# A context tile taken out of the expert loop and gathered beside the latents' mixer

## What is computed

```python
h = rms_norm(x, g_norm1) * (1 + sc1) + sh1
x = x + ga1 * (concat(short_conv(h), bidirectional_mLSTM(h)) @ w_out)
h = rms_norm(x, g_norm2) * (1 + sc2) + sh2
# PEER, per token: 8 heads choose 16 of 16384 experts each
a = einsum('td,thkd->thk', h, u_tab[e])
x = x + ga2 * einsum('thk,thkd->td', gate * gelu(a), v_tab[e])
y = rms_norm(x, g_final)
```

## Time and profile before

| | us |
|---|---|
| median of 3 runs (lowest, highest) | 3864.77 (3859.73, 3868.69) |
| the profiled execution: its time | 3873.35 |
| its span, first to last instruction | 3871.2 |
| busy: PE, DVE, POOL, ACT | 3283.1, 2431.6, 1290.4, 978.3 |

### The profile page before, as it was taken

The page is one execution under the profiler, slowest core; times in us unless marked ns, Lnnn a source line. Parts: engine busy times, 40 slices in busy tenths (PEclk is TensorE's granted clock), DMA queues, the critical chain, the costliest instruction groups (busy, mean ns, idle before and its releaser), DMA issues.

```text
span 3871.2 us, 38481 instructions
## 1 busy us (share of the span) xinstructions
PE 3283.1 (85%) x10672; PEld 1647.3 (43%) x10672; DVE 2431.6 (63%) x6016; ACT 978.3 (25%) x2384; POOL 1290.4 (33%) x1174
## 2 busy tenths in 40 slices
PE   6999999479878888887888798788878878887887
PEld 4555555334434434443443344344334433443443
DVE  3433233466767766776677667666766767676776
ACT  1301101122322222232223222222222222222222
POOL 0000000144434443443444344344434434443443
PEclk8999999799999999999999899999999999999999
DMA  8010100799999999999999999999999999999998
GB/s 354 23 37 29 41 25 9 296 397 401 409 373 400 410 406 369 405 401 377 407 406 404 376 403 405 370 411 405 408 374 388 397 378 403 408 403 374 404 404 330
DMA packets 197995, 1298.57 MB, mean 335 GB/s; under 512 B 22336, under 2 KB 34944, under 8 KB 48768
## 3 DMA queue, kind: packets, MB, share of 16 engines
q0 software_dynamic: 165888, 1208.03, 77.0%
q1 hardware_dynamic: 31872, 87.83, 6.0%
HBM read 1285.76 MB, written 10.01 MB: 335 GB/s over the span
## 4 chain that ended last, share of the span: by engine, by line
DVE 23%; PE 20%; DMA 19%; issue 14%; ACT 3%; DVEq 2%; POOL 1%; ACTq 0%; POOLq 0%
DMA uv<-in_uv,expert 19%; PE acc L1062 15%; DVE uv L1250 8%; PE mix L1026 4%; DVE wt L1202 2%; ACT gelu L1112 2%; POOL uv L989 1%; DVE work L1186 1%; DVE work L1182 1%; DVE picked L1189 1%; ACT diag L1117 1%; DVE ind L1150 1%; DVE ind L1143 1%; DVE work L1144 1%; DVE pos L1165 1%
## 5 line engine op out<-in xcount | busy, mean ns | idle before, releaser
L1062 PE MATMUL acc<-uv,diag 128*128 128x512 f32 x4608 | 2210.9, 629 | 445.1 <-ACT diag L1117 445.0
L989 POOL DMA_INDIRECT uv<-in_uv,expert x1152 | 1286.8, 1117 | 1859.1 <-PE acc L1062 1588.5
L1250 DVE CUSTOM_DVE_ANT_0 uv<-uv,h 128x1024 f32<-128x1024 f32 x1152 | 1385.6, 1221 | 484.5 <-DMA uv<-in_uv,expert 481.3
L1062 PEld LDWEIGHTS acc<-uv,diag 128*128 128x128 f32 x4608 | 884.4, 199 | 1658.0 <-issue 966.4
L1117 ACT ACTIVATE diag<-ident,wt 128x128 f32<-128x128 f32 x1152 | 423.2, 397 | 576.3 <-PE acc L1062 417.1
L1112 ACT ACTIVATE gelu<-dot 128x2 f32<-128x2 f32 x576 | 117.4, 204 | 1409.7 <-DVE dot L1250 1408.5
L489 PE MATMUL region<-hT_then_w_out,w 128*128 128x512 f32 (+1 forms) x1344 | 453.2, 499 | 4.1 <-DVE seen L756 4.1
L1003 PE MATMUL ps_q<-h2T,wq 128*128 128x128 f32 x2336 | 292.7, 286 | 56.2 <-issue 55.0
L1003 PEld LDWEIGHTS ps_q<-h2T,wq 128*128 128x128 f32 x2336 | 289.7, 202 | 93.8 <-issue 93.8
L489 PEld LDWEIGHTS region<-hT_then_w_out,w 128*128 128x128 f32 x1344 | 228.1, 196 | 228.4 <-issue 223.2
L1202 DVE SCALAR_TENSOR_TENSOR wt<-gelu,rz,ex 128x2 f32<-128x2 f32 x576 | 127.3, 221 | 270.5 <-ACT gelu L1112 270.5
(11 more groups left out here) (203 smaller groups left out, 1563.4 us busy)
## 6 DMA issues: line engine op xcount, KB each, us to landing
wada<-in_w_ada SPq DMA_DIRECT2D x12, 2048.0 KB, 17.0
uv<-in_uv,expert POOLq DMA_INDIRECT x1152, 9.9
w<-in_w_in SPq DMA_DIRECT2D x28, 512.0 KB, 3.3
wq<-in_wq SPq DMA_DIRECT2D x1, 7168.0 KB, 26.8
next_h<-scratch_cat SPq DMA_DIRECT2D x10, 512.0 KB, 11.7
next_x<-in_x SPq DMA_DIRECT2D x10, 512.0 KB, 8.4
gate<-scratch_mod SPq DMA_DIRECT2D x10, 512.0 KB, 11.0
xt<-in_x SPq DMA_DIRECT2D x9, 512.0 KB, 19.0
```

Of the source, the lines that this page charges most:

```text
L989: nc.gpsimd.indirect_dma_start(out=uv[:, k % RING, :], out_offset=None, in_=t["uv"], in_offset=bass.IndirectOffsetOnAxis(ap=expert[:, h % ...
L1062: last = nc.tensor.matmul(acc[:, a * BANK:(a + 1) * BANK], diag[:, k % DIAG, :], uv[:, k % RING, D + a * BANK:D + (a + 1) * BANK], start=( ...
L1250: last = nc.vector.tensor_tensor_reduce(out=uv[:, k % RING, 0:D], in0=uv[:, k % RING, 0:D], in1=h2[:], scale=1.0, scalar=0.0, op0=ALU.mult ...
```

## The change

A new `context_stage` stands between modulation and mixer. It makes the gates of all nine tiles and takes the context tile alone through all seven projections of all heads (28 of 8 matmuls on 128 columns, weights loaded head 3 first, head 0 last), conv, both mLSTM directions (zero start, so no recurrence), output projection, residual, second norm, queries, scores and all eight choices on DVE. Each pick gets two row numbers, 2e and 2e + 1, in a view of the expert table with 4 KB rows. Among this PE also projects the latents' first q (ahead of the gate columns), v and k (among the choices).

The mixer then has eight tiles (1024 columns) and no prologue, and its heads are written out. POOL gathers the context's 256 rows of 4 KB into six slots, each as soon as DVE has read the slot's last row. DVE takes them at six places of each head: 128 dots, one GELU over all dots on ACT in the third head, and 128 sums `acc = row * weight + acc` with `acc` in PSUM.

```diff
+    BESIDE = ((14, 8, 6, 5, 8, 14), (14, 8, 6, 5, 8, 14), (18, 8, 6, 5, 8, 14), (14, 8, 6, 5, 8, 14))
+    GELU_HEAD = 2
...
+        acc = own.enter_context(nc.psum_tensor("c_acc", [P, D], F32))
...
+                for k in range(2 * PICKS):
+                    if k >= RS:
+                        pool.wait_ge(c_read, k - RS + 1)
+                    side, pick = divmod(k, PICKS)
+                    nc.gpsimd.indirect_dma_start(
+                        out=ring[:, k % RS, :], out_offset=None, in_=t["uv_rows"],
+                        in_offset=bass.IndirectOffsetOnAxis(ap=s["cexpert"][:, side, pick:pick + 1], axis=0),
+                    ).then_inc(c_rows_in[k % RS], 16)
...
+                        dve.wait_ge(c_rows_in[k % RS], ROWS_BASE + 16 * (k // RS + 1))
+                        row = ring[:, k % RS, :]
+                        if k < PICKS:
+                            nc.vector.tensor_tensor_reduce(out=row, in0=row, in1=s["ch2"][:], scale=1.0, scalar=0.0,
+                                                           op0=ALU.mult, op1=ALU.add,
+                                                           accum_out=dot[:, k:k + 1]).then_inc(c_read, 1)
+                        else:
+                            nc.vector.scalar_tensor_tensor(out=acc[:], in0=row, scalar=wt[:, k - PICKS:k - PICKS + 1],
+                                                           in1=acc[:], op0=ALU.mult, op1=ALU.add).then_inc(c_read, 1)
+                            dve.drain()
...
                     mask_rows(0)
+                    beside(h, 0)
                     arguments(0)
                     weights(0)
                     mask_rows(1)
+                    beside(h, 1)
                     chain(0)
+                    beside(h, 2)
...
+                    beside(h, 3)
                     chain(1)
+                    beside(h, 4)
...
                                             ALU.mult).then_inc(h_ready, 1)
+                    beside(h, 5)
                     dve.wait_ge(jobs_done, job_done(h, "hT"))
...
-                with dve.Fori(0, HEADS - 1) as h:
+                for h in range(HEADS):
                     body(h)
-                body(HEADS - 1)
+                context(2 * PICKS)
+                context_end()
```

`context_end` waits for three vectors that SP loads after the last sum, applies gate, residual and final norm, and SP stores the context's `y` and waits for it. The third head's ACT queue waits for all 128 dots ahead of that head's exponentials. The expert loop keeps its form with eight tiles, all latents, with the latents' vectors alone in its prologue, and no gate load per tile:

```diff
-                with pool.Fori(0, NT) as i:
+                with pool.Fori(0, NL) as i:
...
-                    sp.wait_ge(acc_read, i + 1)
-                    sp.dma_start(gate2[:], t["mod"][(i + 7) // 8, 5 * D:6 * D].partition_broadcast(P))\
-                        .then_inc(gate2_in, 16)
```

More of the change, by code:

```diff
@@ L276, in left_out @@
 def left_out(h, name, region=None):
-    if not isinstance(h, int) or h < HEADS - 1:
+    if h < HEADS - 1:
         return 0
@@ L345, in mixer_stage @@
[L345 to L356, removed]
@@ L668, in body, with context_gelu @@
                     evict_next("v")
-                with act.Fori(0, HEADS - 1) as h:
+                def context_gelu():
+                    act.wait_ge(c_read, PICKS)
+                    nc.scalar.activation(gelu[:], dot[:], ACT.Gelu).then_inc(c_gelued, 1)
+                for h in range(HEADS):
                     body(h)
-                body(HEADS - 1)
+                act.wait_ge(c_meansq2, 1)
+                nc.scalar.activation(fst[:, 2:3], fst[:, 1:2], ACT.Sqrt).then_inc(c_rooted2, 1)
             @block.vector
@@ L695, in _ @@
-                last.then_inc(free[region_of("v")], 1)
-                dve.wait_ge(g_log, 1)
-                for d in range(2):
-                    nc.vector.scalar_tensor_tensor(out=gf[d], in0=gf[d], scalar=0.0, in1=lg[d], op0=ALU.min,
-                                                   op1=ALU.subtract)
-                dve.drain()
-                for d in range(2):
-                    run = (lambda a: a) if d == 0 else (lambda a: a[:, ::-1])
-                    end = P - 1 if d == 0 else 0
-                    nc.vector.tensor_tensor_scan(out=run(bsum), data0=keep[:], data1=run(gf[d]), initial=0.0,
-                                                 op0=ALU.mult, op1=ALU.add)
+                nc.vector.memset(acc[:], 0.0)
@@ L708, in _, with beside, context_end @@
+                def beside(h, place):
+                    context(sum(map(sum, BESIDE[:h])) + sum(BESIDE[h][:place + 1]))
+                def context_end():
+                    dve.wait_ge(c_last_in, 48)
+                    nc.vector.tensor_tensor(gate2, acc[:], gate2, ALU.mult)
                     dve.drain()
-                    nc.vector.tensor_tensor(gmb[:, d], gi[d], bsum, ALU.subtract)
+                    nc.vector.tensor_tensor(x1, x1, gate2, ALU.add)
                     dve.drain()
-                    nc.vector.tensor_tensor_scan(out=run(top[:]), data0=low[:], data1=run(gmb[:, d]), initial=0.0,
-                                                 op0=ALU.add, op1=ALU.max)
+                    nc.vector.tensor_tensor_reduce(out=gate2, in0=x1, in1=x1, scale=1.0, scalar=0.0,
+                                                   op0=ALU.mult, op1=ALU.add, accum_out=fst[:, 0:1])
@@ L723, in _ @@
-                    src = slice(1, NT - 1) if d == 0 else slice(NT - 1, 1, -1)
-                    dst = slice(2, NT) if d == 0 else slice(NT - 2, 0, -1)
-                    nc.vector.tensor_tensor_scan(out=ends[:, 2, dst], data0=ends[:, 0, src], data1=ends[:, 1, src],
-                                                 initial=m0[:, d:d + 1], op0=ALU.max, op1=ALU.add)
-                    dve.drain()
-                    before = ends[:, 2, :].unsqueeze(2).to_broadcast([HEADS, NT, P])
-                    nc.vector.tensor_tensor(chunks(top[:]), chunks(top[:]), before, ALU.max)
```

901 lines of the change are left out of this document (683 added, 218 removed).

## The result

The changed kernel takes 3770.41 us (median of 4 runs, 3767.37 to 3773.87) where the kernel before takes 3864.34: a ratio of 0.9757, 95% interval 0.9740 to 0.9774. The forecast was 3747 in a range of 3705 to 3840, so sign and range held; the time is 23 us above the forecast, and the gain is 94 us where some 118 was forecast.

What follows compares the result with a forecast made beforehand. DMA engines bound the expert loop; the mixer leaves them idle. Span 3871.2 - 345.8 (tile) + 160 (context stage) + 67.6 (mixer) = 3753.0, with 2.15 around it 3755.2, scaled to the median 3747 us; range 3705 to 3840.

Steps and rivals of the forecast that it cites:

- The tile that goes: Expert loop: one of its tiles disappears, saving 345.8 us.
- The context stage: New serial stage before the mixer: everything up to the mixer's bodies ends at 313.6 instead of 153.7, 160 us later.
- The head without picks: Mixer at eight tiles: a head falls from 143.5 to 127 us before any picks are added.
- A burst of 14 dots: DVE at a mixer head's end: six dots at 1.14 us and eight at 1.8, 21.5 us in all.
- The wait at the heads' ends: Mixer: PE waits 10 us for the turned head behind a burst of dots, 5.5 to 14 at the bounds.
- The other 14 lie beside PE's turns and og projection (19.5): Mixer heads: these dots hide beside PE work; with the bursts of 5 to 8, 1 us more.
- The last head: Mixer: the fourth head, with four projections less to hide picks behind, takes 126 us.
- The two-pass rival: DVE's sums, read and written in PSUM, take 2.5 us each; time 3885 us, chance 0.08.
- Never held: Mixer's gathers: rows arrive 1.24 us apart throughout; stage 597, time 3729 us, chance 0.14.
- Slow supply: Mixer's gathers: 2.3 us for each dot and sum; stage 703, time 3835 us, chance 0.13.
- A longer context stage: Stage before the mixer: choices wait for the projections laid among them; time 3784 us, chance 0.11.
- No gain from shorter rows: Gathers: 4 KB rows take 2.5 us like 8 KB ones; stage 742, time 3874 us, chance 0.04.

Runs made afterwards that it cites:

- e6: Changed kernel with eight slots instead of six for the gathered rows; 3755.7 us, ratio 0.9719 to the kernel before.
- e8: Changed kernel with square root first on ACT, h in PSUM, eight slots, later weight loads and redistributed picks; 3712.9 us, ratio 0.9586 to the kernel before.
- e1: Changed kernel with the 256 gathers, their dots, the GELU and the sums left out; 3640.2 us.
- e4: Changed kernel with all picks moved behind the four mixer heads, the GELU too; 4008.2 us.
- e3: Changed kernel with ACT's square root for the norm of h ahead of the eviction of the next head's q; 3743.0 us, ratio 0.9675 to the kernel before.
- e7: Changed kernel with SP's loads of the second head's q, k and v weights moved behind the first head's k by q; 3781.4 us.
- e2: Changed kernel with the dots reading h from PSUM, picks in their places; 3758.5 us, ratio 0.9715 to the kernel before.
- e5: Changed kernel with all picks behind the heads and operands swapped: dots read h from PSUM, sums accumulate in SBUF; 3997.0 us.

## Why the prediction was right, and where it was off

**The tile that goes, -345.8: right.** A tile takes 346.8. Whether the 1.0 belongs to the change can't be told: kernels with the very same loop show 345.4 (e6) to 348.8 (e8) a tile, eight times which is 28 us. The loop's +8.9 lies within that, and so does the dropped gate load, which I put at 0 to 10; it was not tried alone.

**The context stage: forecast 7.2 too long.** The 28 projections took 50.2, not 52.4, and the output product 15.9, not 16.5. The mLSTM's estimate was near: its product starts at 193.0, with 197.7 forecast. Eight choices at 9.4 were forecast at 9.3. (In the recorded rival 8 x 4.5 is 36, not 37.)

**The mixer: mechanism right, one term missing, one mis-sized.**
- The head without picks: 127 with 1.3% on it, 129 in e1. Right.
- "A burst of 14 dots is 6 in hand at 1.14 and 8 at 1.8: 21.5." It took 21.65; the terms add to 21.2. The pitch is not a steady one, though: while dots run on rows in hand, gathers pass every 2.3 us and at times later, then every 1.25 to 1.3 once DVE waits, and 1.43 is the mean of a long run (e4). The bound "at worst every second dot lets one pass" did not hold: the gather at 460.75 took 3.12 us.
- The wait at the heads' ends: 10 forecast, 12.6, 13.5 and 10.3 measured, within its bounds of 5.5 to 14. Its 4.3 us from q's copy to h are 4.1 in the first head. That this order of ACT's queue was a choice, and most of the wait its price, is what the prediction did not see (e3).
- **The term that was mis-sized:** "The other 14 lie beside PE's turns and og projection (19.5)", at 1 us for the whole row of places. PE waited there 8.6, 3.6 and 6.4. The burst has to end in 19.5 us and takes 21.5 by my own figure. In the first head, besides, the first row lands after 7.8 us instead of 4.2, and 2.5 of that are the weight loads that SP issues at the same moment, which I did not count (5.3 without them, e7). With the waits at the ends this makes the heads 149.6, 144.7 and 146.6 instead of 138, 138 and 144.
- The last head: 126 forecast, 131.4 measured.
- The sums: 1.42 taken, 1.38 measured, in and out of PSUM in one pass. The two-pass rival, at 2.5, is out, and the 32 behind the heads took 44.4 where 45.4 stood. The context's end took the 15.5 that stood there, in part by luck: the terms as written (6, six times 1.3, 2.5) add to 16.3, and the loads took 6.9, the operations 5.9, the store 2.7.

**The rivals.** "Never held" at 3729 was priced 18 below the forecast; e2 makes it true and gains 12. "Slow supply" at 2.3 for dots and sums holds only for some gathers of a burst of dots; no gather under the sums was held. "A longer context stage" fell with choices at 9.4. "No gain from shorter rows" fell with dots 1.30 apart (e5). What was said against it had the trace wrong: before 86 us, 1544 of the 3824 packets are of 8 KB or more, and the weights are in those, not in pieces of 2 KB. In the earlier trace rows, too, the nines begin with the ninth slice, not the eighth.

The Trainium skill's rule on two non-bf16 SBUF sources (Vector Engine (DVE) Microarchitecture Reference, section Points that are easy to get wrong), which I had weighed against a row, can be held against e5 too: the sums with two f32 SBUF sources take 1.284 us, those with one 1.290, so no run here shows the halving.

## What to carry to other kernels

Work laid into another stage's idle engine costs what it makes the bound engine wait for: price it place by place, against what that engine does in the very stretch, and count every transfer issued at the same moment. Before moving the work, look at what stands ahead of the place in each queue: one line in ACT's order was worth more (27 us) than either change to the supply of rows that gained (12 in e2, 15 in e6). If POOL's gathers run beside DVE work, keep one operand of that work in PSUM, and compare it in the gather's line, by its maximum.

## What the runs showed that was not expected

- The longest hold of a gather does not follow the supply alone: 3.13 us in the changed kernel, 4.28 with eight slots (e6), 5.12 with six and the square root first (e3), while about as many gathers take over 1.2 us in each (52, 53 and 53 of 256). Why some pass after one dot and others after four is open; with h in PSUM none is held (e2, e8).
- The clock after a wait. PE's granted clock behind the wait of 12.56 us at the second head's start (changed kernel, columns as above, the clock is third from the end) is 0.58 for the first 4 us, 0.50 being the lower level of 1.2 GHz, then 1.00. Behind the wait of 13.51 it is 0.50 in the first 4 us, and in e3, behind waits of 4.39 and 2.95, still 0.50 and 0.60; behind the waits of 1.47 in e1 it is 1.00 at once. The og projection pays 1.0 to 2.1 us for it. A wait is not needed, though: in e1 the cg projection at 456.73 (last row) starts at 0.50 after one of 0.17, right behind the matmuls that spread gate rows from 4 partitions; every projection right behind such a spread, in every run, starts at 0.50 to 0.65.

```profile
456.20:460.50 4.30, 4.30 (x12) 2.84 (x13) 4.30 (x7) 2.31 (x2) 2.33 (x2) 0.58 0.92 313
460.50:472.50 12.00, 12.00 (x29) 5.28 (x28) 8.72 (x16) 0.00 (x0) 9.92 (x7) 1.00 0.92 312
...
456.73:460.73 4.00, 4.00 (x5) 1.82 (x6) 1.92 (x3) 1.86 (x2) 0.00 (x0) 0.50 0.00 0
```

- The loop's tile varies by 1% between executions of the same code (345.4 to 348.8), which is more than several of the edits are worth: the stretches of the mixer, not the medians, tell those apart.
